# Extra matrix products into an unread bank, in eight tiles of the first expert half

## The reference

```python
def peer(xn, w_pq, sub_k1, sub_k2, u_tab, v_tab):
    q = (xn @ w_pq).reshape(B, T, PEER_HEADS, PEER_DK)
    s1 = einsum('bthd,kd->bthk', q[..., :half], sub_k1)
    s2 = einsum('bthd,kd->bthk', q[..., half:], sub_k2)
    v1, i1 = top_k(s1, 16);  v2, i2 = top_k(s2, 16)
    ...                       # 16 of the 256 sums, their expert numbers eid, softmax weights g
    a = gelu(einsum('nd,ned->ne', xb, u_tab[eb]))
    return einsum('ne,ned->nd', a * gb, v_tab[eb])
```

## Time and profile before

| what | value |
|---|---|
| time, median of 2 runs | 4086.65 us (4086.31 to 4086.99) |
| span of the profiled execution | 4078.4 us |
| TensorE busy | 3974.5 us, 97% of the span |
| VectorE, ScalarE busy | 2372.5 us (58%), 2067.9 us (51%) |
| mean granted TensorE clock | 0.990 |
| read from memory | 712.52 MB, 177 GB/s over the span |

### The profile page before, as it was taken

The page is one execution under the profiler, slowest core; times in us unless marked ns, Lnnn a source line. Parts: engine busy times, 40 slices in busy tenths (PEclk is TensorE's granted clock), DMA queues, the critical chain, the costliest instruction groups (busy, mean ns, idle before and its releaser), DMA issues.

```text
span 4078.4 us, 82496 instructions
## 1 busy us (share of the span) xinstructions
PE 3974.5 (97%) x33876; PEld 3926.6 (96%) x33876; DVE 2372.5 (58%) x3435; ACT 2067.9 (51%) x3122; POOL 43.9 (1%) x65
## 2 busy tenths in 40 slices
PE   7999999999999998999999998999999999999998
PEld 7999999999999998999999998999999999999998
DVE  7555565554444556444665666997765555555555
ACT  6554554455555444444654444447764444444443
POOL 1000000000000000000000000000000000000000
PEclk9999999999999998999999999999999999999999
DMA  4545455545555554444335444555555556665553
GB/s 176 186 166 174 168 182 180 191 159 189 192 195 194 188 194 151 169 164 139 128 135 182 170 155 136 183 194 179 179 196 195 190 191 217 215 211 192 193 190 131
DMA packets 111189, 726.09 MB, mean 178 GB/s; under 512 B 11296, under 2 KB 11424, under 8 KB 29184
## 3 DMA queue, kind: packets, MB, share of 16 engines
q1 hardware_dynamic: 105904, 701.55, 50.2%
q0 software_dynamic: 5072, 21.50, 1.6%
HBM read 712.52 MB, written 10.49 MB: 177 GB/s over the span
## 4 chain that ended last, share of the span: by engine, by line
PE 95%; DVE 2%; ACT 2%; issue 1%; DMA 0%; DVEq 0%; SPq 0%; ACTq 0%
PE ps L502 19%; PE ps L510 19%; PE ps L503 19%; PE ps L561 9%; PE ps L563 9%; PE ps L568 9%; PE ps L590 1%; PE ps L1002 1%; PE ps L531 1%; PE ps L625 1%; PE ps L532 1%; PE ps L533 1%; PE ps L643 1%; ACT wh L1064 1%; DVE tmp L1734 0%
## 5 line engine op out<-in xcount | busy, mean ns | idle before, releaser
L1669 DVE TENSOR_TENSOR wl<-raw,wh 128x1024 fp32r<-128x1024 f32 x1328 | 1618.3, 1226 | 1476.2 <-ACT wh L1064 1471.1
L1064 ACT ACTIVATE wh<-raw 128x1024 fp32r<-128x1024 f32 x1328 | 1402.7, 1060 | 1757.0 <-PE ps L561 607.5
L502 PE MATMUL ps<-x,wh 128*128 128x256 f32 x6656 | 1590.8, 281 | 27.3 <-DVE x L1728 25.1
L503 PE MATMUL ps<-x,wh 128*128 128x256 f32 x6656 | 1575.7, 279 | 0.0
L502 PEld LDWEIGHTS ps<-x,wh 128*128 128x128 f32 x6656 | 1260.8, 189 | 36.5 <-issue 30.1
L503 PEld LDWEIGHTS ps<-x,wh 128*128 128x128 f32 x6656 | 1260.7, 189 | 0.6
L510 PE MATMUL ps<-x,wl 128*128 128x256 f32 x6656 | 902.2, 278 | 4.3 <-DVE wl L1669 4.3
L510 PEld LDWEIGHTS ps<-x,wl 128*128 128x128 f32 x6656 | 828.1, 189 | 4.5 <-DVE wl L1669 4.5
L561 PE MATMUL ps<-xkh,wh 128*128 128x256 f32 x3328 | 779.4, 277 | 9.4 <-DVE xkl L1680 8.4
L563 PE MATMUL ps<-xkl,wh 128*128 128x256 f32 x3328 | 778.7, 277 | 0.0
L561 PEld LDWEIGHTS ps<-xkh,wh 128*128 128x128 f32 x3328 | 626.8, 188 | 10.8 <-DVE xkl L1680 9.3
(11 more groups left out here) (350 smaller groups left out, 2365.2 us busy)
## 6 DMA issues: line engine op xcount, KB each, us to landing
raw<-in_w_in SPq DMA_DIRECT2D x184, 1024.0 KB, 4.8
raw<-in_expert_u SPq DMA_DIRECT2D x128, 1024.0 KB, 4.8
raw<-in_expert_v SPq DMA_DIRECT2D x128, 1024.0 KB, 4.8
raw<-in_w_ffn_gate SPq DMA_DIRECT2D x44, 1024.0 KB, 4.7
raw<-in_w_ffn_up SPq DMA_DIRECT2D x44, 1024.0 KB, 4.7
raw<-in_w_ffn_down SPq DMA_DIRECT2D x44, 1024.0 KB, 4.7
raw<-in_w_out SPq DMA_DIRECT2D x32, 1024.0 KB, 4.8
raw<-in_w_branch SPq DMA_DIRECT2D x16, 1024.0 KB, 4.9
```

Source lines behind the costliest of these rows:

```text
L502: begin(mm(o, wh[:, j, c], x_h[:, kc, :], start=kc == 0, stop=False), kc % 8 == 0)
L503: mm(o, wh[:, j, c], x_l[:, kc, :], start=False, stop=False)
L1064: f(wh[:, u % 4, 0:width], raw[:, ring, c:c + width], ACT.Copy).then_inc(*k.up("hi"))
L1669: v.tensor_tensor(wl[:, u % 4, 0:width], raw[:, ring, c:c + width], wh[:, u % 4, 0:width].bitcast(F32), ALU.subtract).then_inc(*k.up("lo"))
```

## The change

`tile_T` gets an argument `extra`. Where it is given, the function `unread` is called behind the first half's low products. For c = 3, 6, ..., 24 of the first expert half it issues 16 or 17 products; all start and stop their own accumulation in bank 7, which nobody reads. Eight forms occur: all 16 chunks with high and low activations side by side, 512 columns (`stacked`); the same for 8 chunks in turn with a product of the low weights, 256 columns; the activations as the stationary operand and 512 or 256 columns of the high weights streaming (`turned`); 384 columns of the activations; and rows of 512 with one of 384 ahead or behind. All of them use the half's weights `wh[:, j]` or `wl[:, j]` that the tile has just used.

```diff
-            def tile_T(b, reader="a", x_h=xh, x_l=xl, spare=None, spare_at=1):
+            def tile_T(b, reader="a", x_h=xh, x_l=xl, spare=None, spare_at=1, extra=None):
...
                         m = mm(o, wl[:, j, c], x_h[:, kc, :], start=False, stop=kc == KC - 1)
+                    if extra is not None and kc0 == 0:
+                        unread(extra, j)
                 m.then_inc(*k.up(f"full_{reader}{b}"))
                 fresh.clear()
+
+            def unread(c, j):
+
+                def stacked(kc, n=2 * T):
+
+                    mm(ps[:, 7, 0:n], wh[:, j, kc % 8 * P:(kc % 8 + 1) * P], x2[:, kc].rearrange("p s t -> p (s t)")[:, 0:n],
+                       start=True, stop=True)
+
+                def turned(part, kc, side, at_col, n):
+
+                    mm(ps[:, 7, 0:n], x2[:, kc, part, side * P:(side + 1) * P], wh[:, j, at_col:at_col + n],
+                       start=True, stop=True)
+
+                reserve(7)
+                if c == 3:
+                    for kc in range(16):
+                        stacked(kc)
+                elif c == 6:
+                    for kc in range(8):
+                        stacked(kc)
+                        mm(ps[:, 7, 0:T], wl[:, j, kc * P:(kc + 1) * P], xh[:, kc, :], start=True, stop=True)
+                elif c == 9:
+                    for kc in range(16):
+                        turned(kc % 2, kc // 2, 0, 0, 512)
+                elif c == 12:
+                    stacked(15, 384)
+                    for kc in range(16):
+                        stacked(kc)
+                elif c == 15:
+                    for kc in range(8):
+                        turned(0, kc, 0, 0, 512)
+                        turned(0, kc, 0, 512, 512)
+                elif c == 18:
+                    for kc in range(16):
+                        turned(kc % 2, kc // 2, 0, kc % 4 * T, T)
+                elif c == 21:
+                    for kc in range(16):
+                        stacked(kc, 384)
+                elif c == 24:
+                    for kc in range(16):
+                        stacked(kc)
+                    stacked(15, 384)
...
             for c in range(HALF):
-                tile_T(c % 2, spare=7 if c == 1 else None)
+                tile_T(c % 2, spare=7 if c == 1 else None, extra=c if 2 < c < 25 else None)
```

## The result

| what | before | after |
|---|---|---|
| time, median of 2 runs | 4086.65 us (4086.31 to 4086.99) | 4110.18 us (4108.03 to 4112.33) |
| ratio | | 1.0058, 95% interval 1.0042 to 1.0074 |
| span of the profiled execution | 4078.4 us | 4110.6 us |

What follows compares the result with a forecast made beforehand. PE's issue pace was taken as the bound. 88 x 220 ns, 24 x 113.3 ns and 18 x 170 ns sum to 25.1 us; added to 4086.65 us this gave 4111.8 us, range 4107 to 4119 us.

Steps and rivals of the forecast that it cites:

- Cover: none: Behind the added products up to the end: no wait of PE hides any of their 25.1 us.
- the index chain: Tile 30, where PE waits for the indices: the chain starts from PE, moves with it, and the wait gets no worse.
- The price of 512 columns: The 88 added products of 512 columns: 220 ns each, between 212 and 227, together 19.4 us.
- the upper bound: Added 512-column products: 227 ns each, by the same 57 ns step that led from 256 to 384 columns.
- The first rival: Tiles behind the added rows: pace falls from 113.3 to 117.9 ns, 2.0 us (4113.8) or 6.9 us (4118.7); chance 0.09.
- The argument against it: Against a fallen pace: a 384-column product in this stage has 113 ns behind it, and more columns should disturb less.
- the +-2 us: Behind the wait ahead of the value rows: the granted clock of 0.59 may move the time by this much.
- The better pace in the routing: The 31 routing tiles are spared 117.9 ns: 6.8 us come back, 4105 us; chance 0.06 including a better pace before routing.
- the sign that the prediction had named: Routing stage: the first half tile behind the second routing pair takes 2.83 us again.
- Full 32-bit prices: Added products run like the sum of squares, 1.69 ns a column: 98 us, 4185 us, 2.4% slower; chance 0.02.
- overlap: Consecutive wide products overlap, so 512 columns cost no more than 256: sum 15.8 us, time 4102.5 us; chance 0.02.

Runs made afterwards that it cites:

- the mended kernel: The changed kernel with one more 384-column product behind the rows of tiles 6 and 15; 4113.37 us, ratio 1.0068 to the kernel before.

## Why the prediction was right, point by point

**PE's pace is the bound, and added products are paid in full.** Right. The change's own cost is 27.7 us between the two marks around the tiles and next to nothing (0.2 us) comes back behind; the mended kernel's 27.2 us in time (22 to 34) fit. "Cover: none" is right too: the wait ahead of the value rows stayed at 3.23 us, the index chain moved with PE, and the 13 products put into that wait were free.

**The price of 512 columns was mis-sized.** 220 ns were taken, within 212 to 227; the rows show 233 (229 in tile 15). The 88 products cost 20.5 us and not 19.4, and the upper bound was too low. It drew a straight line from 113.3 through one product of 384 columns at 170 ns; sixteen in a row took 173 each, and the line through that price ends at 233. So the single distance held no surcharge for the shift of widths, the reason given for going below the bound, but was 3 ns short of the price in a row. 24 products of 256 columns took 2.8 (2.7), 18 of 384 columns 3.1 (3.1). So 26.4 us stand against the 25.1 forecast.

**The pace was left out of the sum.** It fell behind two of the eight rows: six tiles, 288 products x 4.5 ns = 1.3 us, which with 26.4 gives the 27.7. The first rival had its place and about its size for a few tiles (2.0 us), but only part of its reason: the row of pairs left the slower pace and so did one turned row (tile 15), while the two other turned rows, entered at the slower pace, left the better one. The argument against it, that more columns should disturb less, was wrong: a single 512-column product turns the pace over. That the plain rows of sixteen cost no pace here isn't explained by their count, since in two other runs such rows turned the slower pace into the better one.

**The time came nearer than the sum, by luck.** The forecast's time was 1.6 us off, its sum 2.6 us below the cost that the traces show. The forecast's 25.1 us lie between the 23.5 of the two medians and the 27.7 of the traces. The difference between these is within what executions of one kernel differ by: the clock granted behind PE's waits moves one kernel's time over some 9 us, more than the +-2 us that were allowed for, and two runs of each don't settle it.

**Rivals.** The better pace in the routing came for three tiles, against the sign that the prediction had named, and gave back 0.2 us: routing took 247.7 us against 247.9. The rival's 6.8 us for all 31 tiles was mis-sized too, as it left out that the routing products themselves take longer at that pace; 7.44 against 7.32 to 7.40 us a tile makes an estimate of 2 to 3 us. Full 32-bit prices and overlap are out: 130 records, at 233 ns for 512 columns.

## What to carry to other kernels

Where one engine is busy for 100% of a stretch and waits for nothing in it, an added instruction costs its full distance between starts; the same instruction in a wait of that engine costs nothing, and may even be worth something if it keeps the clock up. Take that distance from a row of the same type and width; where only a single product stands in the trace, let the range reach beyond the line drawn through it (here 170 ns for one, 173 in a row, and 233 instead of 227 at the next width). Before a fraction of a per cent is explained by a change, compare marks inside the trace: ahead of the change, behind it, and to the end. And before a rule from one run is carried on, look for rows in the other runs that break it.

## What the runs showed of the hardware

- A stream of 32-bit products has two paces, 113.3 and 117.9 ns for 256 columns, that lasted from tile to tile until another shape came. In one run one, three or five plain products of 512 columns turned one into the other, both ways (9 of 9 cases), and two, four or eight changed nothing (5 of 5); but rows of sixteen that were entered at the slower pace left the better one (2 of 2).
- 32-bit products of 512 columns cost 225 to 236 ns in every place, bank and order tried; 16-bit ones of the same width started 216 ns apart.
- Behind one and the same wait of PE of 3.2 us the granted clock over 4 us was 0.50 to 0.59 in six profiled executions and 1.00 in two. Behind a wait of 7.7 us at a norm it was 0.73 to 0.80 over 25 us in nine executions, and 1.00 in the one with products that nobody reads in the wait.
